# Scan to out-projection in a hybrid decoder layer: earlier loads and weight cuts, a third place for a tile, sums of squares inside a unit

## What is computed

```python
def gated_group_rmsnorm(y, z, w):
    g = (y * jax.nn.silu(z)).astype(jnp.float32)
    shp = g.shape
    g = g.reshape(*shp[:-1], SSM_GROUPS, shp[-1] // SSM_GROUPS)
    g = g * lax.rsqrt(jnp.mean(jnp.square(g), axis=-1, keepdims=True) + EPS)
    return g.reshape(shp).astype(z.dtype) * w
...
    ssm = gated_group_rmsnorm(y, z, ssm_norm)
    return jnp.concatenate([att, ssm], axis=-1) @ w_out
...
        h = h + rmsnorm(mix, norm_mix_post[layer])
        f = jnp.square(jax.nn.relu(rmsnorm(h, norm_mlp_pre[layer]) @ w_mlp_up[layer])) @ w_mlp_down[layer]
        h = h + rmsnorm(f, norm_mlp_post[layer])
```

## Time and profile before

| | us |
|---|---|
| median of three runs | 1765.79 |
| the profiled execution, its own time | 1773.68 |
| its span | 1771.9 |
| TensorE busy (matmuls) | 1643.6 (93%) |
| VectorE busy | 816.1 (46%) |
| ScalarE busy | 490.0 (28%) |
| POOL busy | 810.3 (46%) |

### The profile page before, as it was taken

How to read it: one execution, slowest core, us unless ns; L and a number is a source line. 1 busy time by engine, 2 the same in 40 slices (tenths; PEclk the granted TensorE clock), 3 DMA queues, 4 the chain that set the end, 5 groups by cost and what they waited for, 6 DMA issues and landing times.

```text
span 1771.9 us, 23019 instructions
## 1 busy us (share of the span) xinstructions
PE 1643.6 (93%) x8311; PEld 1404.1 (79%) x8311; DVE 816.1 (46%) x1398; ACT 490.0 (28%) x1002; POOL 810.3 (46%) x780
## 2 busy tenths in 40 slices
PE   2999999978899998799996899999999999999997
PEld 2999998857787887578885687888888888888886
DVE  4465515165766666567765665322222222222225
ACT  4222312233444444345553333010202020201022
POOL 4452544154556542824321424646464646464624
PEclk8999999999999999799998899999999999999999
DMA  5333522235544444478856742111111111111123
GB/s 173 93 114 116 177 54 66 65 93 141 157 135 144 120 141 119 157 283 292 293 189 236 254 156 95 48 48 48 47 47 47 48 46 53 47 53 42 54 79 134
DMA packets 165399, 208.43 MB, mean 118 GB/s; under 512 B 18896, under 2 KB 117040, under 8 KB 165328
## 3 DMA queue, kind: packets, MB, share of 16 engines
q1 hardware_dynamic: 165328, 207.52, 36.2%
HBM read 138.16 MB, written 69.30 MB: 117 GB/s over the span
## 4 chain that ended last, share of the span: by engine, by line
PE 47%; DVE 3%; issue 2%; DMA 2%; ACT 2%; POOL 1%; SPq 0%; POOLq 0%; DVEq 0%; ACTq 0%
PE ps L2270 19%; PE ps L2256 18%; PE ps L2160 5%; PE ps L2116 1%; PE ps L2140 1%; PE ps L2225 1%; DVE m_mix L2598 1%; PE ps L2127 0%; ACT m_junk L2400 0%; DMA s_aTlo<-d_ssmlo 0%; DMA d_h<-m_h 0%; PE ps L2093 0%; PE ps L2092 0%; PE ps L2107 0%; DVE m_mix L2612 0%
## 5 line engine op out<-in xcount | busy, mean ns | idle before, releaser
L164 POOL TENSOR_TENSOR ring<-stage,zero 128x512 fp32r<-128x512 f32 (+2 forms) x191 | 205.6, 1077 | 298.5 <-PE ps L2270 109.0
L2270 PE MATMUL ps<-ring,f1hi 128*128 128x512 f32 x1024 | 315.2, 389 | 0.0
L2256 PE MATMUL ps<-hmThi,ring 128*128 128x512 f32 x960 | 298.0, 389 | 0.0
L166 POOL TENSOR_TENSOR ring<-stage,ring 128x512 fp32r<-128x512 f32 (+2 forms) x191 | 248.5, 1301 | 15.0
L2270 PEld LDWEIGHTS ps<-ring,f1hi 128*128 128x128 f32 x1024 | 192.2, 188 | 39.9
L2256 PEld LDWEIGHTS ps<-hmThi,ring 128*128 128x128 f32 x960 | 180.2, 188 | 37.4
L2270 PE MATMUL ps<-ring,f1lo 128*128 128x512 f32 x512 | 199.2, 389 | 0.0
L2256 PE MATMUL ps<-hmTlo,ring 128*128 128x512 f32 x480 | 186.7, 389 | 0.0
L2641 DVE TENSOR_TENSOR acc<-ps,acc 128x512 f32<-128x512 f32 x128 | 88.0, 691 | 212.1 <-PE ps L2270 210.2
L2432 ACT ACTIVATE relu<-ps 128x512 f32<-128x512 f32 x64 | 38.2, 597 | 514.5 <-PE ps L2256 514.5
L2632 DVE TENSOR_TENSOR ps<-ps,relu 128x512 f32<-128x512 f32 x64 | 44.8, 699 | 215.1 <-ACT relu L2432 215.1
(11 more groups left out here) (368 smaller groups left out, 3392.8 us busy)
## 6 DMA issues: line engine op xcount, KB each, us to landing
stage<-w_mlp_up SPq DMA_DIRECT2D x64, 256.0 KB, 2.6
stage<-w_mlp_down SPq DMA_DIRECT2D x64, 256.0 KB, 2.5
stage<-w_in SPq DMA_DIRECT2D x40, 256.0 KB, 2.7
stage<-w_out SPq DMA_DIRECT2D x32, 256.0 KB, 4.7
xt<-x SPq DMA_DIRECT2D x8, 512.0 KB, 8.6
d_xT<-xdT SPq DMA_DIRECT2D x8, 512.0 KB, 3.3
d_x<-x_tok SPq DMA_DIRECT2D x8, 512.0 KB, 4.6
d_zT<-zs SPq DMA_DIRECT2D x16, 256.0 KB, 2.3
```

The source lines that it names most:

```text
L164: pool.tensor_tensor(hi, src, k.zero[:, 0:1].broadcast_to([P, width]), ALU.add).then_inc(k.sem(fam + "_hi"), 1)
L166: pool.tensor_tensor(lo, src, hi.bitcast(F32), ALU.subtract).then_inc(k.sem(fam + "_cut"), 1)
L2256: mm = pe.matmul(ps[:, bank_of(n, first), :], block_w[:, P * j:P * j + P], HM[b][:, kk, at], start=(kk == 0 and a == 0 and b == 0), stop=( ...
L2270: mm = pe.matmul(ps[:, 2 + n % 4, :], f1[a][:, j, P * t:P * t + P], W[b][:, HALF + 2 * j + c, :], start=(j == 0 and a == 0 and b == 0), st ...
```

## The change

It touches only `phase_rest`.

- **Weights.** Blocks 20 to 23 are asked for in chunk 6 rather than after the scan. Blocks 16 to 19 are cut in chunk 6 (before: 16 and 17 there, 18 and 19 in chunk 7), 20 to 23 in chunk 7, 24 to 27 ahead of the last half tile, 28 to 31 behind it.
- **Tile 0** is loaded as soon as its place is free, ahead of the store of tile 6 and of the loads of z and the attention half. The store of tile 6 moves behind blocks 24 to 27.
- **Third place.** Tile 2 goes into `xh[0]`, which the scan has left. Tiles 3 to 7 alternate between the two old places. So tile 3 follows unit 2, tile 4 unit 3, tile 5 unit 7, tile 6 unit 9 and tile 7 unit 11.
- **Loads in the tile loop.** Tile t + 3 is asked for ahead of the loads of the attention half and of x.
- **Sums of squares** of tiles 6 and 7 move from between units 1 and 2 into the middle of unit 2, and the wait for their reading into the middle of unit 3.
- The row of norm weights moves to another place in memory, and its load ahead of the store of tile 7.

```diff
     assert o <= o_acc
-    wrow, o = m.at("m_wrow", [P, D], F32, o_gT)
-    junk, o = m.at("m_junk", [P, D], F32, o)
+    wrow, _ = m.at("m_wrow", [P, D], F32, k.o_relu)
+    junk, o = m.at("m_junk", [P, D], F32, o_gT)
     assert o <= o_xw
+    EXTRA = 2
+    def parts_of(t):
+        return [x[:, :].rearrange("p (k n) -> p k n", n=P) for x in xh[0]] if t == EXTRA else [x[:, t % 2 if t < EXTRA else (t - 3) % 2, :, :] for x in aT]
+    def ssm_in(t):
+        return ("m_x_in", 32) if t == EXTRA else (f"s_at_in{t % 2}", 16 * NT + 32) if t < EXTRA else (f"s_at_in{(t - 3) % 2}", 16 * NT + 32 * ((t - 3) // 2 + 2))
+    def used_before(t):
+        return unit[t - 3 if t < 5 else t - 2, 1] + 1
     h, o = m.at("m_h", [P, 2, D], F32, o_acc)
...
             def load_tile(src, t):
...
                     sp.dma_start(aT[i][:, t % 2, :, :].bitcast(F32), src[i][t]).then_inc(sem(f"s_at_in{t % 2}"), 16)
+            def load_ssm(t):
+                for a, src in zip(parts_of(t), k.d_ssm):
+                    sp.dma_start(a.bitcast(F32), src[t]).then_inc(sem(ssm_in(t)[0]), 16)
             def store_mix(t, c):
...
                     load_cT(t + 1)
+                if t == LAST:
+                    sp.wait_ge(sem("s_mix"), nth_mix[LAST - 1, 1] + 1)
+                    sp.wait_ge(sem("s_sent"), 32 * (LAST - 1))
+                    load_ssm(0)
+                    sp.wait_ge(sem("s_gz"), 2 * LAST)
+                    load_z(LAST)
+                    load_mix(0)
+                    load_mix(1)
+                    break
                 if t:
...
                     load_z(t)
-                    if t < LAST:
-                        sp.wait_ge(sem("s_sq"), 2 * t)
-                        load_skip(t + 1)
-                if t == LAST:
-                    load_mix(0)
-                    load_mix(1)
-                    sp.wait_ge(sem("s_mix"), nth_mix[LAST - 1, 1] + 1)
-                    load_tile(k.d_ssm, 0)
-                    break
+                    sp.wait_ge(sem("s_sq"), 2 * t)
+                    load_skip(t + 1)
                 sp.wait_ge(sem("s_stp"), t + 1)
...
                     store_mix(LAST, 0)
+                    blocks(RING + STAGES, RING + KD)
                 store_mix(t, 1)
-            blocks(RING + STAGES, RING + KD)
             sp.wait_ge(sem("s_mix"), 2 * NT)
-            load_tile(k.d_ssm, 1)
+            load_ssm(1)
             blocks(RING + KD, RING + KD + STAGES)
+            store_ssm(LAST - 1)
             store_mix(LAST, 1)
+            load_ssm(EXTRA)
+            blocks(RING + KD + STAGES, RING + KD + 2 * STAGES)
             sp.wait_ge(sem("s_t1"), NT)
             load_h(0)
-            blocks(RING + KD + STAGES, RING + KD + 2 * STAGES)
             for c in range(2):
...
             load_h(1)
+            sp.wait_ge(sem("s_sqr"), 2 * NT)
+            sp.dma_start(wrow[:, :], io["norm_mix_post"][0].partition_broadcast(P)).then_inc(sem("m_w_in"), 16)
             store_ssm(LAST)
-            sp.wait_ge(sem("s_sent"), 32 * NT)
-            sp.dma_start(wrow[:, :], io["norm_mix_post"][0].partition_broadcast(P)).then_inc(sem("m_w_in"), 16)
             def next_tile(t):
                 if t < NT:
-                    sp.wait_ge(sem("m_mm"), unit[t - 2, 1] + 1)
-                    load_tile(k.d_ssm, t)
-            next_tile(2)
+                    sp.wait_ge(sem("m_mm"), used_before(t))
+                    if t == LAST - 1:
+                        sp.wait_ge(sem("s_sent"), 32 * NT)
+                    load_ssm(t)
             next_tile(3)
+            next_tile(4)
             for t in range(NT):
                 store_h(t)
+                if t >= 2:
+                    next_tile(t + 3)
                 if t + 2 < NT:
...
                     up_blocks(0, STAGES)
-                if t:
-                    next_tile(t + 3)
                 if t == NT - 3:
...
             def mm_unit(i):
                 t, c = UNITS[i]
-                pe.wait_ge(sem(f"s_at_in{t % 2}"), 16 * NT + 32 * (t // 2 + 1))
+                s = parts_of(t)
+                pe.wait_ge(sem(ssm_in(t)[0]), ssm_in(t)[1])
                 if i == 0:
...
                     pe.wait_ge(sem("s_mixc"), 2 * NT)
-                    pe.wait_ge(sem("s_ssv"), NT)
                 if i >= 4:
...
                 for g in range(GROUPS):
+                    if i == 2 and g:
+                        pe.wait_ge(sem("s_y1"), 4 * NT)
+                        squares(LAST - 1, 3, 0)
+                        squares(LAST, 3, 4)
+                    if i == 3 and g:
+                        pe.wait_ge(sem("s_ssv"), NT)
                     for kk in range(4 * g, 4 * g + 4):
...
                         for a, b in PASSES:
-                            mm = pe.matmul(ps[:, unit_banks(i)[g], :], aT[a][:, t % 2, kk, :], W[b][:, KD * c + kk, :],
+                            mm = pe.matmul(ps[:, unit_banks(i)[g], :], s[a][:, kk, :], W[b][:, KD * c + kk, :],
                                            start=(kk == 4 * g and (a, b) == (0, 0)), stop=(kk == 4 * g + 3 and a == 1))
...
             mm_unit(1)
-            pe.wait_ge(sem("s_y1"), 4 * NT)
-            squares(LAST - 1, 3, 0)
-            squares(LAST, 3, 4)
             TURNS = {5: 0, 6: 1, 8: 2, 10: 3, 12: 4, 14: 5}
...
                 expo(t, 1)
+                if t == LAST:
+                    w_cuts(RING + STAGES, RING + STAGES + 2)
                 if t:
...
                 if t == LAST:
-                    w_cuts(RING + 2, RING + STAGES)
+                    w_cuts(RING + STAGES + 2, RING + KD)
                 expo(t, 2)
...
                 w_hi(t, 2)
-                if t == LAST:
-                    w_cuts(RING + STAGES, RING + STAGES + 2)
                 expo(t, 3)
                 if t == LAST:
-                    w_cuts(RING + STAGES + 2, RING + KD)
                     mix_out(t, 1)
...
                 squares(t, 0)
+                if t == LAST - 1:
+                    w_cuts(RING, RING + STAGES)
                 if t < LAST:
                     mix_out(t, 1)
-                if t == LAST - 1:
-                    w_cuts(RING, RING + 2)
             for t in range(NT):
...
             act.wait_ge(sem("s_mix"), 2 * NT)
-            w_cuts(RING + KD, RING + KD + 2)
+            w_cuts(RING + KD, RING + KD + STAGES)
             squares(LAST, 1)
-            w_cuts(RING + KD + 2, 2 * RING)
+            w_cuts(RING + KD + STAGES, 2 * RING)
             act.wait_ge(sem("g_v"), 1)
...
                 mul(t, 1)
+                if t == LAST:
+                    w_cuts(RING + STAGES, RING + STAGES + 2)
                 dve.wait_ge(sem("s_off"), t + 1)
...
                 else:
-                    w_cuts(RING + 2, RING + STAGES)
+                    w_cuts(RING + STAGES + 2, RING + KD)
                 skipped(t, 1)
...
                     dve.tensor_tensor(sth[1][:, :], state[:, :], sth[0][:, :].bitcast(F32), ALU.subtract).then_inc(sem("s_stlo"), 1)
-                else:
-                    w_cuts(RING + STAGES, RING + KD)
                 skipped(t, 2)
...
                 if t == LAST - 1:
-                    w_cuts(RING, RING + 2)
+                    w_cuts(RING, RING + STAGES)
             for t in range(NT):
                 chunk(t)
-            w_cuts(RING + KD, RING + KD + 2)
+            w_cuts(RING + KD, RING + KD + STAGES)
             summed(LAST, 1)
             low_half(LAST, 1)
-            w_cuts(RING + KD + 2, 2 * RING)
+            w_cuts(RING + KD + STAGES, 2 * RING)
             dve.wait_ge(sem("s_ssq"), NT)
```

## The result

| | before | after |
|---|---|---|
| median of four runs each, side by side, us | 1765.74 | 1752.45 |
| lowest to highest | 1764.34 to 1766.09 | 1750.14 to 1757.48 |
| the profiled execution, its own time | 1773.68 | 1757.48 |
| its span | 1771.9 | 1755.7 |

The changed kernel takes 0.9921 of the time before, with an interval of 0.9897 to 0.9945: 13.9 us less by this ratio (the medians differ by 13.3). Faster was right; the size is little more than half of the 24.4 us forecast, and 1752.45 lies above the range of 1735 to 1749.

The account below looks back on a forecast made before the run. It took the MLP as bound by matmuls, and the stretches before 1060 us by TensorE's waits and low clock. Savings of 20.1 + 4.3 = 24.4 us gave 1741.4 us, own range 1738 to 1745, with rivals 1735 to 1749.

Parts of the forecast that it names:

- the base: Whole kernel: the 24.4 us saving, built on one 1773.68 us profile, was taken off the 1765.79 us median.
- stage A: Scan's last matmul to the first turned tile, 61.1 us before: the turn starts at 971.9 instead of 991.99, saving 20.1 us.
- the landing of a store: Before the factor: tile 6's store, behind four blocks, leaves at 934.8 and lands 4.1 us later, near 939.2.
- S to M: From the scan's last matmul to the MLP's first matmul, the two forecast stretches together; savings of 20.1 and 4.3 us.
- The term for the wait before unit 8: Between first turned tile and MLP: the 3.2 us wait goes, as tile 4 is asked for straight after unit 3.
- R: When the factor of the gated norm is ready: forecast at 953.8 us, before at 971.63; bounds 950 to 958.
- R to T: From the gated norm's factor to the first turned tile: the normalisation chain takes 18.0 us, as before.
- Slower: Rival: tile 6's store behind four loads delays copy, cuts and factor; saving gone if 24 us later; chance 0.02.
- Stage B: First turned tile to the MLP's first matmul: 63.2 us instead of 67.5, saving 4.3 us.
- What follows shifts unchanged: After 1060 us, in the MLP: the 3.1 us wait for tile 6 stays and the rest only shifts.
- The prediction's own gauge: Clock after waits: first two matmuls take 1.22 us after 9.9 and 0.73 after 1.2, so short waits cost little.
- The normalisation is the bound: Rival: from the factor to the MLP everything takes 87.8 us as before; 17.8 saved, 1748.0 us; chance 0.13.

Follow-up runs that it names:

- store_first: Changed kernel with the store of tile 6 sent one step earlier on SP, ahead of the next tile and blocks 24 to 27: 1748.42 us, 0.9886 of before.
- quiet_queue: Changed kernel with tile 6's store first, MLP blocks 4 to 7 earlier, tile 2 and attention halves 0 and 1 behind blocks 28 to 31: 1753.79 us, 0.9912.
- two_places: Changed kernel without the third place for a tile and with SP's loop in its old order: 1756.99 us, 0.9931 of before.
- after_again: The changed kernel, unedited, profiled a second time: median 1753.76 us, 0.9918 of before.
- before_again: The kernel before, unedited, profiled a second time: 833.9 us from the scan's last matmul to the end.
- third_place_only: The kernel before with only the third place for a tile and the new order of SP's loop: 1766.3 us, 0.9983 of before.
- extra_late: Changed kernel with tile 6's store first, MLP blocks 4 to 7 one tile earlier, and tile 2 loaded behind tile 7's store: 1747.75 us, 0.9862.

## Why the prediction was wrong

Three steps of the prediction failed: the base from which the saving was taken, one term of stage A (the landing of a store), and the statement that nothing changes behind the MLP's first matmul.

**The base, 5.9 us of the 24.4 (3.9 against the mean of all three profiles of before).** The first step that failed is the one that says "the saving lies in waits, so I take it off this median". I measured 128.5 us from S to M in an execution 7.9 us above the median, and took the whole saving off the median. Two executions of the same kernel at 1767.46 and 1765.45 us need 122.7 and 122.6. The term for the wait before unit 8, with its low clock, was a price that these two do not pay in full. How often it is paid is open: in the later comparisons the kernel before had medians of 1769.76 to 1772.79, so executions like the first are not rare.

**Stage A, up to R.** The mechanism held: first tile early, the store of tile 6 behind four loads, the copy held by one buffer, cuts, last blocks. The four cuts took 4.78 us where I had 5.0, R to T 18.0 where I had 18.0, the wait before the first turned tile 2.57 where I had 2 to 3. The mis-sized term is the landing of the store: I took 4.1 us, from a median over stores with less ahead of them, and it took 8.7. The factor came 27.0 and 25.9 us after S, where 22.9 was forecast; store_first, which takes the store off the path, gives 21.5. It is the mechanism of the rival *Slower*, with 3 to 4 us at R instead of the 24 that it would have needed. Counted from S this still lies within the prediction's own bounds for R, 950 to 958, that is 19.1 to 27.1 us.

The Trainium skill, "SBUF — State Buffer", section "Who interferes with whom", has a VectorE instruction with two SBUF inputs contend with a GpSimd instruction that reads SBUF. The rows agree again, with 4.78 us for four cuts there, against 2.73; the forecast had allowed for it with 5.0.

**Stage B** was 63.2 by forecast and is 61.5 and 60.5: no wait in it, where 0.8 was allowed for tile 7, and less low clock than allowed. S to M as a whole was forecast as 104.2 and measured as 106.6 and 104.4; the late factor and the short stage B partly cancel, which is luck. So up to the MLP's first matmul the forecast was nearly right as a time, and wrong as a difference.

**After 1060, the term of nothing.** "What follows shifts unchanged" failed. From M to the end the kernel before needs 712.5, 711.2 and 712.0 us, the changed one 715.5 and 715.4: 3 to 4 us given back. The prediction put nothing here, without a row for it. The wait before the turned tile 6 is 4.3 us, not 2.5 to 3.1, and the clock falls after it. The stretch right behind the end of that wait, in after (columns as in the earlier trace rows) and in the profile of before (TensorE alone, then clock, DMA share and GB/s):

```profile
1055.60:1062.10 6.50, 6.41 (x22) 5.46 (x23) 2.64 (x10) 3.77 (x8) 4.20 (x4) 0.60 0.68 221
```

```profile
1073.60:1080.00 6.40, 6.37 (x32) 1.00 0.65 220
```

The granted clock is 0.60 of full in the one, that is mostly the lower level of 1.2 GHz, and 1.00, 2.4 GHz throughout, in the other. By the timelines the next 24 matmuls of the MLP take 7.37 us instead of 5.72. The Trainium skill, "TensorE: Matmul & The Clock Gate", section "What's actually happening", has the slow clock as the default that activity releases. The rows agree that waits bring it back: after this one the granted clock is 0.60. Which wait does, its length alone does not tell. At this same place 3.13 us in before were followed by full clock, and 3.13 in quiet_queue and 2.65 in two_places by 6.50 and 7.32 us for those 24 matmuls. The prediction's own gauge, the first two matmuls behind a wait, was too short as well: in before, behind the 1.8 us wait for the sums of squares, the first two take 0.71 us, and yet the granted clock from 962.0 to 966.3 is 0.60.

What made tile 6 late can be narrowed down. In all fourteen profiles 19.7 us lie between VectorE's addition of unit 14 and the turned tile 6, and unit 14 ends 6.3 to 6.4 us ahead of M. So M to H grows by just as much as that addition starts later behind its unit: 0.2 to 0.8 us in the three profiles of before, 2.2 and 2.9 in after and after_again. Before, VectorE still waited for TensorE there, as this addition of before_again for tile 7's first half does:

```profile
1043.01 1.54 DVE L2598 SCALAR_TENSOR_TENSOR m_mix<-ps,dend,m_mix 128x512 f32<-128x512 f32 x2 [2.98 <-PE ps L2225]
```

Without the waits for tiles TensorE arrives sooner than VectorE's chain, which now waits 2.16 us for tile 7's half of the attention and 1.55 for MLP blocks; so the addition of unit 14 starts 2.2 us after that unit's end at 1033.8. SP asks for both loads behind the store of a residual tile, which is the end of VectorE's own chain. The runs bear this out as far as they go: third_place_only has the 2.15 us wait for that half and the longer M to H, two_places has neither. In quiet_queue and extra_late, though, VectorE waits 3.3 us for that half, and M to H is only 14.2 and 15.1: how much of the delay is due to this one load is not shown. Earlier blocks alone took 0.6 us off TensorE's wait. An earlier load of the half was not tried. It is the rival *The normalisation is the bound*, in one place and not over the whole stage.

**The sum again.** 24.4, less 5.9 for the base, 1.3 for S to M (the mean of 106.6 and 104.4 less 104.2) and 3.9 behind M (715.5 and 715.4, less the mean of 711.2 and 712.0) leaves 13.3. The traces give 834.2 - 820.9 = 13.3 from S to the end, against the same two profiles of before. With all three profiles as the base it is 15.6. The runs give 13.9 and 14.5 by the two ratios, and 13.3 and 16.0 by the medians. The interval of the first ratio runs from 9.7 to 18.2 us, so an agreement to 1 us is luck. No one of these terms alone would have taken 1741.4 out of the range up to 1749; together they do.

What stays open: why the clock falls after one pause of three microseconds and not after another, what makes the addition of unit 14 late, whether less load in front makes the last blocks land sooner, and why S itself moves by 9.6 us over fourteen profiles.

## What to carry to other kernels

Take the base of a forecast from more than one profiled execution, above all where a wait hangs on a margin of 1 us: a stage measured in a run above the median can't be subtracted whole from the median. Where one instruction marks a stage, see whether it waited for something else: in quiet_queue the first addition stood 1.9 us behind the factor. Where an edit moves a store behind loads on one queue, don't cost it by the median landing of stores that had less ahead of them, and look at who waits for its buffer; here one line's place was worth 5 us. When a change removes an engine's waits, follow the next engine past the end of the stage, since what it catches up with (here the loads behind VectorE's chain) takes part of the gain back.

## What was not expected of the hardware

The second half of the same store, 512 KB, landed in 5.3 us when sent first (store_first), and in 8.7 and 7.8 us behind tile 1 and four blocks (after, after_again). After waits of the same length before the same tile, 3.13 us, the clock stayed full in before and fell in quiet_queue. And the stretch up to S, nearly the same code in all fourteen profiles, ends between 924.9 and 934.5 us.
